# Gate rows computed as columns, diagonal constants moved to VectorE ahead of the loads, last tile's half sums on GpSimd, new priorities and addresses, in an eight-core hybrid trunk layer

## The chip, the cores and the metric

The kernel runs on all 8 cores of one Trainium2 chip. Each core computes one denoising request (1024 latent tokens) and two context requests (2 x 256 tokens); all cores run the same program and exchange nothing. The metric is the device time in microseconds of the slowest core. Before the change it is 719.71 us, the median of 3 runs (719.04 to 720.16).

Each core has a matrix engine (TensorE, PE), VectorE (DVE), ScalarE (ACT), GpSimd (POOL) and SyncE (SP). SP does nothing but issue DMAs. POOL computes and also issues the DMAs that convert float32 weights to bfloat16 on the way.

## What is computed

One layer of a flow-matching backbone. With `mod = silu(cond) @ w_ada + b_ada` split in six vectors of 1024 (shift1, scale1, gate1, shift2, scale2, gate2):

```python
h    = x * (1 + sc1) + sh1
proj = h @ w_in                          # q,k,v,g of 4 retention heads; z,x,B,C,dt of the SSD heads
ret  = silu(g) * rms_norm(bidirectional retention(q, k, v))     # latent q,k get a 2D rotary
ssd  = rms_norm(bidirectional SSD(silu(conv5(x,B,C)), dt) * silu(z)) * ssd_norm_w
x    = LN1(ALPHA * x + g1 * (concat(ret, ssd) @ w_out))
x    = LN2(ALPHA * x + g2 * ((silu(h2 @ w_gate) * (h2 @ w_up)) @ w_down)),  h2 = x * (1 + sc2) + sh2
```

Context tokens (group GA, tiles 8 to 11) use one shared conditioning vector, latent tokens (group GB, tiles 0 to 7) their own. So every modulation vector exists twice per core.

## The kernel before, in words

**The program is a list that a planner orders.** The Python code creates operations (class `Op`) in program order, each with the engines that may run it, a cost in us, a priority (`P.level`, lower goes first, corrected by the table `LEVELS` under the stage's name and level) and its dependencies. Dependencies on SBUF are kept in cells of 32 bytes (`View.cells`). `Prog.schedule` then plays the program with these costs: at each moment an engine takes the ready operation with the lowest priority number. What comes out is a fixed order for every engine; on the chip each engine works through its own list and waits on semaphores. A matmul that takes a new PSUM bank also waits for whatever else the readers of that bank need (`Prog.whole`), so that a bank is never held by something that can't be drained. In the planner's clock a DMA queue moves 318 KB per us (SP) or 290 KB per us (POOL).

**Addresses.** `Prog.place` gives every buffer an address. Two buffers may share bytes if their lifetimes in the planner's time don't meet, with a margin `slack` in us; `PLACED` is a list of addresses tried first. The first operation on a later buffer waits for all operations on the earlier one.

**Stages in order.**
- Start (tag "start"): SP loads, in this order, `cols` (per-partition constants), two halves of `w_ada` slab 2, the first half of `xT` chunk 2 (the context tokens, transposed), of `w_in` slab 0, then `cst` (396 columns: identity, triangle, ones, small tables), the first half of `w_in` slab 1, of `xT` 0, `smalls` (48 values for every partition), `xT` 1, slab 3 of `w_ada`, and the second halves. ACT, DVE and POOL cast the pieces to bfloat16 (L781, L733). `mod_cols` makes scale1 as columns: 32 matmuls with 2 moving columns. The scaled tokens `hA` are then multiplied with `w_in` half by half (`proj_xbc`; the halves are summed on DVE, L756).
- `diagw` (eight 128 x 640) and `dI` (two 128 x 512) are diagonal matrices, made from the identity in `cst` by ten `tt` on DVE or POOL at level 3. `diagw` turns the five-tap convolution into matmuls.
- `sh1` (level 0.6): shift1 as columns from slabs 0 and 1 of `w_ada`, which POOL loads one after the other when `xT` has landed; then shift1 times `w_in` for the bias of the convolution. The convolutions wait for that.
- The context heads, context SSD blocks ("ssd", "blk8" to "blk11"), `gate_row(0, half)` for gate1, `mod2` for shift2 and scale2, the context output stage ("out1"), and then the latent SSD ("ssdB", "blk0" to "blk7"), the latent heads ("head0", which need the rotary table `rope`, 1 MB, loaded by SP behind the last context head), "out0".
- The feed-forward of the latent tokens from 447 us on, in it `gate_row(1, half)`; then the down projection, first the context tiles, then the latent ones, tile 7 last through `last_tile` in column slices of 512, 256 and 256.

**What the change touches.** `gate_row` computes a gate as a row: 8 matmuls with 2 stationary columns (`scv3`) and 512 moving ones, a DVE add of the bias row `gb` (its own SP DMA, which waits for the `w_ada` slab), and a 2 x 512 store into the DRAM scratch `gsc`. `gate_load` reads one 1024-wide row of `gsc` back, broadcast to all partitions, for each group. In `last_tile`, when slice 1 is done, two `ts` on 128 x 1 values (L762, L764) add the two first sums and sums of squares on DVE. In `down` the layer norm's multiply and add (`ln2`) go to POOL, except for tiles 5 and 6, where the planner may choose DVE. `tt` is L756, `ts` L762/L764, `stt` L770, `cp` L781, matmuls L708, transposes L711, DMAs L194.

## Time and profile before

| | us |
|---|---|
| median of 3 runs | 719.71 (719.04 to 720.16) |
| the profiled execution, its own time | 724.19 |
| its span on the slowest core (core 5) | 723.1 |
| spans of the eight cores | 711.1 to 723.1 |
| PE busy (share of the span) | 673.9 (93%) |
| DVE, POOL, ACT busy | 401.2 (55%), 343.7 (48%), 328.2 (45%) |
| DMA share in 0 to 90 us | 0.8 to 1.0 |

The span runs from a core's first to its last instruction; 1.1 us of the profiled execution lie around it. All cores run the same instructions in the same order, so a difference between cores is a difference in when DMAs land.

### The profile page before, as it was taken

How to read it: one execution, taken by the hardware profiler on the slowest of the kernel's cores; microseconds unless marked ns; L12 is line 12 of the kernel's file. 1: busy time of each engine (PE TensorE's matmuls, PEld its weight loads, DVE VectorE, ACT ScalarE, POOL GpSimd, SP SyncE). 2: the span in 40 equal slices, each digit the busy share in tenths (PEclk: the TensorE clock that was granted, in tenths of full speed). 3: DMA queues.
4: the chain of work that ended last, by engine and by line, in shares of the span. 5: the costliest groups of instructions: out<-in, count | busy, mean ns of one | idle time of the engine just before them, and what ended most of it. 6: DMA issues, size and time to landing. Idle time of an engine off the chain costs nothing.

```text
span 723.1 us, 13450 instructions; the slowest of 8 cores (711.1 to 723.1 us)
## 1 busy us (share of the span) xinstructions
PE 673.9 (93%) x4270; PEld 347.1 (48%) x4270; DVE 401.2 (55%) x811; ACT 328.2 (45%) x517; POOL 343.7 (48%) x385
## 2 busy tenths in 40 slices
PE   0699899997999999999999999999999999999994
PEld 0244664643548444446565455444444444444442
DVE  2788358661598935787777885212111222475566
ACT  2281876786756535867887536111111110132212
POOL 2520516322614778876773321886481000298752
PEclk9999899998998999999999999999999999999998
DMA  8989996999394499655069637594589954021112
GB/s 233 330 281 151 145 160 115 197 204 250 76 243 108 73 144 177 124 96 101 19 161 215 152 103 180 96 167 80 125 185 158 245 162 80 1 88 59 58 60 87
DMA packets 26677, 102.93 MB, mean 142 GB/s; under 512 B 3168, under 2 KB 7264, under 8 KB 21744
## 3 DMA queue, kind: packets, MB, share of 16 engines
q0 software_dynamic: 11232, 49.83, 41.6%
q1 hardware_dynamic: 15376, 52.24, 22.1%
q8 instruction: 36, 0.59, 0.3%
q14 instruction: 33, 0.27, 0.1%
HBM read 136.40 MB, written 15.48 MB: 210 GB/s over the span
## 4 chain that ended last, share of the span: by engine, by line
PE 79%; DMA 8%; DVE 5%; issue 4%; ACT 2%; POOL 1%; SPq 1%; DVEq 0%; POOLq 0%; ACTq 0%
PE psum L708 77%; DMA arena<-cstf 6%; DVE arena L756 2%; DMA arena<-w_h 2%; ACT arena L733 2%; PE psum L711 2%; DVE arena L770 1%; DVE arena L781 1%; SPq L194 1%; POOL arena L756 1%; DVE arena L790 1%; POOL arena L194 0%; ACT L733 0%; DVE arena L762 0%; DVEq L610 0%
## 5 line engine op out<-in xcount | busy, mean ns | idle before, releaser
L708 PE MATMUL psum<-arena 128*128 128x512 bf16 (+7 forms) x4174 | 663.5, 316 | 38.1 <-ACT arena L733 23.9
L708 PEld LDWEIGHTS psum<-arena 128*128 128x128 bf16 (+2 forms) x4174 | 335.9, 100 | 362.7 <-issue 86.4
L756 POOL TENSOR_TENSOR arena<-arena 128x512 f32<-128x512 f32 (+5 forms) x215 | 272.9, 1286 | 177.8 <-DVE arena L764 70.9
L733 ACT ACTIVATE arena<-psum 128x512 bf16<-128x512 f32 (+3 forms) x208 | 118.5, 579 | 188.6 <-PE psum L708 174.6
L733 ACT ACTIVATE arena<-arena 128x512 bf16<-128x512 f32 (+8 forms) x160 | 109.7, 706 | 164.6 <-DVE arena L770 86.4
L756 DVE TENSOR_TENSOR arena<-arena,psum 128x512 bf16<-128x512 bf16 (+1 forms) x120 | 80.9, 684 | 144.2 <-PE psum L708 131.7
L756 DVE TENSOR_TENSOR arena<-psum,arena 128x512 bf16<-128x512 f32 (+4 forms) x183 | 111.5, 631 | 59.0 <-PE psum L708 55.2
L733 ACT ACT_TABLE_LOAD x52 | 66.7, 1283 | 21.4 <-PE psum L708 11.0
L756 DVE TENSOR_TENSOR arena<-arena 128x1 f32<-128x1 f32 (+9 forms) x105 | 51.8, 502 | 22.2 <-POOL arena L756 13.6
L194 POOL DMA_DIRECT2D arena<-w_gu x44 | 25.9, 588 | 76.0 <-PE psum L708 69.5
L770 DVE SCALAR_TENSOR_TENSOR arena<-arena 128x512 f32<-128x512 f32 (+2 forms) x77 | 52.9, 697 | 5.0 <-DVE arena L756 0.9
L733 ACT ACTIVATE arena<-psum,arena 128x512 bf16<-128x512 f32 (+2 forms) x59 | 37.3, 650 | 13.4 <-PE psum L711 9.1
L781 DVE CAST arena<-psum 128x512 bf16<-128x512 f32 (+1 forms) x35 | 22.1, 649 | 19.3 <-PE psum L708 19.0
L781 POOL CAST arena<-arena 128x2 bf16<-128x2 f32 (+3 forms) x65 | 19.1, 333 | 20.9 <-DMA arena<-w_in 6.6
L790 DVE TENSOR_SCALAR arena<-arena 128x512 f32<-128x512 f32 (+1 forms) x41 | 23.0, 586 | 0.6
L194 POOL DMA_DIRECT2D arena<-w_h x16 | 8.8, 554 | 28.9 <-PE psum L708 19.0
L194 POOL DMA_DIRECT2D arena<-w_down x4 | 2.1, 528 | 40.8 <-PE psum L708 40.4
L764 DVE TENSOR_SCALAR arena<-arena 128x1 f32<-128x1 f32 (+3 forms) x51 | 9.2, 181 | 20.0 <-ACT arena L733 18.6
L1400 DVE COPY_PREDICATED psum<-arena,psum 128x512 f32<-128x512 uint16 x24 | 16.6, 690 | 5.2 <-PE psum L708 4.9
L781 DVE CAST arena<-arena 128x1024 bf16<-128x1024 f32 (+5 forms) x26 | 13.5, 543 | 9.4 <-DMA arena<-w_ada 6.5
L711 PE MATMUL psum<-arena 128*128 128x128 f32 x96 | 14.8, 299 | 0.6 <-DVE arena L790 0.6
L781 DVE COPY arena<-psum 128x512 f32<-128x512 f32 (+3 forms) x19 | 10.2, 544 | 9.1 <-PE psum L708 8.9
(21 smaller groups left out, 71.3 us busy)
## 6 DMA issues: line engine op xcount, KB each, us to landing
arena<-w_gu POOLq DMA_DIRECT2D x44, 512.0 KB, 7.1
arena<-w_ada POOLq DMA_DIRECT2D x10, 1024.0 KB, 11.9
arena<-w_h POOLq DMA_DIRECT2D x16, 512.0 KB, 10.4
arena<-xT SPq DMA_DIRECT2D x6, 1024.0 KB, 26.1
arena<-x SPq DMA_DIRECT2D x12, 512.0 KB, 10.5
arena<-w_down POOLq DMA_DIRECT2D x4, 1408.0 KB, 15.2
y<-arena SPq DMA_DIRECT2D x11, 512.0 KB, 2.6
arena<-w_ada SPq DMA_DIRECT2D x4, 1024.0 KB, 26.3
```

The lines of the kernel that those rows point to most:

```text
L194: o = self.add({eng: (0.9 if eng == POOL else 0.45, lambda e: e.dma_start(out=R(out), in_=R(in_)))}, [in_], [out], after=after)
L708: return P.add({PE: (c, lambda e: e.matmul(R(out), lhsT=R(lhsT), rhs=R(rhs), start=start, stop=stop))}, [lhsT, rhs], [out])
L711: return P.add({PE: (0.12, lambda e: e.transpose(out=R(out), in_=R(in_), identity=R(ident_f)))}, [in_, ident_f], [out])
L733: fn = lambda e: e.activation(out=R(out), in_=R(in_), func=func, **{k: R(v) for k, v in kw.items()})
L756: fn = lambda e: e.tensor_tensor(out=R(out), in0=R(in0), in1=R(in1), op=op)
L764: fn = lambda e: e.tensor_scalar(out=R(out), in0=R(in0), scalar1=R(s1), scalar2=R(s2), op0=op0, op1=op1)
L770: fn = lambda e: e.scalar_tensor_tensor(out=R(out), in0=R(in0), scalar=R(scalar), in1=R(in1), op0=op0, op1=op1, **{k: R(v) for k, v in kw. ...
L781: alts[g] = (vcost(g, out, [in_], "copy"), lambda e: e.tensor_copy(out=R(out), in_=R(in_)))
L790: lambda e: e.tensor_scalar(out=R(out), in0=R(in_), scalar1=R(scale), scalar2=R(bias), op0=ALU.mult, op1=ALU.add))
L1400: P.add({DVE: (0.7, lambda e, eb=eb, ef=ef, mk_=mk_: e.copy_predicated(R(eb), R(mk_), R(ef)))}, [mk_, ef, eb], [eb])
```

## The change

The priorities and addresses are new as a whole (tables cut here). `cst` is loaded in two parts, its identity and `smalls` ahead of everything but `cols`. The ten diagonal products run on DVE only, at level 0.2 in place of 3; the shift1 section is at level 0.35 in place of 0.6. The first margin tried between lifetimes is 2.0 us in place of 0.2. Gates are computed by `mod_cols` (32 matmuls with 2 moving columns, bias from `cols`), transposed by PE to 8 rows of 128, copied and stored; each is loaded back in two halves. The two sums of the last tile are on POOL, and so is all of the final multiply and add.

```diff
-LEVELS = {('blk0', 1.4): -0.05, ..., ('head0', 1.6): -0.1, ..., ('ssdB', 1.4): 0.02, ..., ('z0', 1.55): 0.5, ...}
+LEVELS = {('blk0', 1.4): -0.5, ..., ('head0', 1.6): -0.06, ..., ('ssdB', 1.4): 0.4, ..., ('z0', 1.55): 1.3, ...}
...
-        for cap, slacks in ((None, (0.2,)), (204000, (3.0, 1.0)), ...
+        for cap, slacks in ((None, (2.0,)), (204000, (3.0, 1.0)), ...
...
+    P.dma(SP, cst[:, 0:128], cf_d[:, 0:128])
+    P.dma(SP, smalls, brow(R_SMALL, 48))
     ada_f32(2)
     for q in range(2):
         xT_load(2, q)
         o_w0 = half_load("w_in0", w0, w_in_d[0], q)
         if q == 0:
-            P.dma(SP, cst, cf_d[:, 0:396])
+            P.dma(SP, cst[:, 128:396], cf_d[:, 128:396])
         o_w1 = half_load("w_in1", w1, w_in_d[1], q)
         xT_load(0, q)
         if q == 0:
-            P.dma(SP, smalls, brow(R_SMALL, 48))
             xT_load(1, 0)
...
+        if name[:2] == "gc":
+            gc[(int(name[2]), int(name[3]))] = m
-        tt(m.rearrange("p (f c) -> p f c", c=2), ps.rearrange("p (f c) -> p f c", c=2),
+        tt(m.rearrange("p (c f) -> p f c", c=2) if name[:2] == "gc" else m.rearrange("p (f c) -> p f c", c=2), ps.rearrange("p (f c) -> p f c", c=2),
...
+    P.level = 0.2
     diagw = P.buf("diagw", 8 * 5 * 128, BF16)
...
-           cols[:, ...].to_broadcast([128, 5, 128]), ALU.mult, (DVE, POOL))
+           cols[:, ...].to_broadcast([128, 5, 128]), ALU.mult)
...
-           smalls[:, 32 + h:36 + h].unsqueeze(2).to_broadcast([128, 4, 128]), ALU.mult, (DVE, POOL))
+           smalls[:, 32 + h:36 + h].unsqueeze(2).to_broadcast([128, 4, 128]), ALU.mult)
...
-    P.level = 0.6
+    P.level = 0.35
     for half in range(2):
         sh1[half] = mod_cols("sh1_%d" % half, half, "mod")
...
     def gate_row(which, half):
-        P.level = LV_BG
-        hs = slice(half * 512, half * 512 + 512)
-        gb = P.buf("gb%d%d" % (which, half), 512)
-        r0 = (R_BG1, R_BG2)[which] + half * 512
-        P.dma(SP, gb[0:2, :], rows_d[0:1, r0:r0 + 512].partition_broadcast(2)..., after=[ada[(4, 10)[which]][1]])
-        P.level = 1.2
-        wv = ada[(4, 10)[which] + half][0].rearrange("p (k n) -> p k n", k=8)
-        ps = P.ps("dense")
-        for kt in range(8):
-            o = mm(ps[0:2, :], scv3[:, kt, :], wv[:, kt, :], kt == 0, kt == 7)
-        P.level = LV_EV
-        gs = P.buf("gst%d%d" % (which, half), 512)
-        tt(gs[0:2, 0:512], ps[0:2, :], gb[0:2, :], ALU.add)
-        P.level = LV_BG
-        gdma[(which, half)] = P.dma(SP, gsc_d[which * 2:which * 2 + 2, hs], gs[0:2, 0:512])
+        P.level = 1.2
+        m = mod_cols("gc%d%d" % (which, half), (4, 10)[which] + half, "dense")
+        P.level = 1.2
+        ps = P.ps("dense", 128)
+        o = tr(ps[0:8, :], gc[(which, half)])
+        P.level = LV_EV
+        gs = P.buf("gst%d%d" % (which, half), 128)
+        cp(gs[0:8, :], ps[0:8, :])
+        P.level = LV_BG
+        r = which * 2 + half
+        gdma[(which, half)] = P.dma(SP, gsc_d[r:r + 1, :].rearrange("a (r p) -> (a r) p", p=128), gs[0:8, :])
         return o
...
     def gate_load(which, g, after):
         b = P.buf("gate%d_%d" % (which, g), 1024)
-        r = which * 2 + g
-        P.dma(SP, b, gsc_d[r:r + 1, :].partition_broadcast(128)..., after=[gdma[(which, 0)], gdma[(which, 1)]] + list(after))
+        for half in range(2):
+            r = which * 2 + half
+            P.dma(SP, b[:, half * 512:half * 512 + 512], gsc_d[r:r + 1, g * 512:g * 512 + 512].partition_broadcast(128)..., after=[gdma[(which, half)]] + list(after))
         return b
...
             if i == 1:
-                ts(s[:, 6:7], s[:, 0:1], s[:, 1:2], ALU.add)
-                ts(s[:, 7:8], s[:, 3:4], s[:, 4:5], ALU.add, EPS, ALU.add)
+                ts(s[:, 6:7], s[:, 0:1], s[:, 1:2], ALU.add, eng=(POOL,))
+                ts(s[:, 7:8], s[:, 3:4], s[:, 4:5], ALU.add, EPS, ALU.add, eng=(POOL,))
...
-                e_ = (DVE, POOL) if t >= 5 and g == GB else (POOL,)
+                e_ = (POOL,)
```

## Rows read from the trace of the kernel before

**Rows 1.** The page: the span, and the engines' busy time, share and instructions

```profile
span 723.1 us, 13450 instructions; the slowest of 8 cores (711.1 to 723.1 us)
PE 673.9 (93%) x4270; PEld 347.1 (48%) x4270; DVE 401.2 (55%) x811; ACT 328.2 (45%) x517; POOL 343.7 (48%) x385
```

**Rows 2.** Spans and granted TensorE clock of single cores

```profile
core 0: 711.1 us, clock 0.988
...
core 5: 723.1 us, clock 0.979
...
core 7: 719.8 us, clock 0.983
```

**Rows 3.** Timeline of PE, core 5: start, us, what, [idle before <- releaser]

```profile
20.79 4.99 PE L708 MATMUL psum<-arena 128*128 128x512 bf16 x16 [5.26 <-ACT arena L733]
29.63 41.80 PE L708 MATMUL psum<-arena 128*128 128x512 bf16 x240 [3.85 <-DVE arena L781]
71.95 0.94 PE L708 MATMUL psum<-arena 128*128 128x2 bf16 x32 [0.53 <-DVE arena L756]
74.19 0.95 PE L708 MATMUL psum<-arena 128*128 128x2 bf16 x32 [1.30 <-DVE arena L781]
76.12 7.66 PE L708 MATMUL psum<-arena 128*128 128x8 bf16 x92 [0.98 <-DVE arena L762]
...
176.24 15.61 PE L708 MATMUL psum<-arena 128*128 128x512 bf16 x116 [4.79 <-DMA arena<-cstf]
```

**Rows 4.** Timeline of all engines, core 5, 0 to 60 us

```profile
1.52 0.89 SPq L194 DMA_DIRECT2D arena<-w_ada  x2
...
21.08 6.16 POOL L756 TENSOR_TENSOR arena<-arena 128x640 bf16<-128x640 f32 x4 [16.57 <-DMA arena<-cstf]
...
22.46 5.46 DVE L756 TENSOR_TENSOR arena<-arena 128x640 bf16<-128x640 f32 x3
...
24.19 1.06 ACT L733 ACTIVATE arena<-arena 128x1024 bf16<-128x1024 f32 x1 [3.54 <-DMA arena<-w_in]
...
27.85 1.52 DVE L781 CAST arena<-arena 128x1024 bf16<-128x1024 f32 x1
...
56.90 0.58 POOL L194 DMA_DIRECT2D arena<-w_ada  x1 [5.46 <-DVE arena L756]
```

**Rows 5.** Windows, core 5: us; PE, PEld, DVE, ACT, POOL busy (x); PEclk, DMA share, GB/s

```profile
4.00:20.00 16.00, 0.99 (x32) 0.94 (x32) 4.01 (x13) 4.94 (x7) 0.51 (x2) 1.00 0.93 284
...
29.60:34.00 4.40, 4.37 (x13) 1.69 (x14) 2.70 (x6) 2.10 (x6) 0.89 (x2) 0.61 1.03 341
...
71.40:85.10 13.70, 9.62 (x158) 7.05 (x157) 7.78 (x26) 11.84 (x19) 10.03 (x53) 0.75 0.98 142
```

**Rows 6.** PE's waits, core 7: us in total, times, longest

```profile
PE psum L708 <- DVE arena L781: 4.6, 3, 2.5
...
PE psum L708 <- DMA arena<-cstf: 1.8, 1, 1.8
```

**Rows 7.** Instructions grouped by form, core 5: busy us, mean ns, then idle before

```profile
L756 DVE TENSOR_TENSOR arena<-arena 128x512 bf16<-128x512 f32 x4 | 2.7, 685 | 0.0
```

**Rows 8.** The page, DMA issues: count, KB each, us to landing

```profile
arena<-w_ada POOLq DMA_DIRECT2D x10, 1024.0 KB, 11.9
```

**Rows 9.** Timeline, core 5: weight loads of two gate rows, and a run of transposes

```profile
494.42 3.11 PEld L708 LDWEIGHTS psum<-arena 128*2 128x2 bf16 x16 [0.42 <-issue]
...
443.26 2.00 PE L711 MATMUL psum<-arena 128*128 128x128 f32 x16 [0.64 <-DVE arena L790]
```

**Rows 10.** Timeline of all engines, core 5, 690 to 724 us

```profile
690.18 1.75 DVE L770 SCALAR_TENSOR_TENSOR arena<-arena 128x512 f32<-128x512 f32 x1
...
709.47 3.46 POOL L756 TENSOR_TENSOR arena<-arena 128x512 f32<-128x512 f32 x2 [1.37 <-ACT arena L733]
...
715.17 0.43 DVE L770 SCALAR_TENSOR_TENSOR arena<-arena 128x256 f32<-128x256 f32 x1
```

**Rows 11.** SP's timeline, core 5: the issue of the rotary table

```profile
148.49 1.49 SPq L194 DMA_DIRECT2D arena<-cstf  x1
```

More of the change, by code:

```diff
@@ L534, in emit @@
         extra = None
-        for cap, slacks in ((None, (0.2,)), (204000, (3.0, 1.0)), (196000, (3.0, 1.0)), (188000, (3.0, 1.0, 0.0)), (180000, (1.0, 0.0))):
+        for cap, slacks in ((None, (2.0,)), (204000, (3.0, 1.0)), (196000, (3.0, 1.0)), (188000, (3.0, 1.0, 0.0)), (180000, (1.0, 0.0))):
             order = self.schedule({}, cap)
@@ L970, in build @@
         tt(diagw4[:, ct, :, :], ident_f.unsqueeze(1).to_broadcast([128, 5, 128]),
-           cols[:, C_CONVW + ct * 5:C_CONVW + ct * 5 + 5].unsqueeze(2).to_broadcast([128, 5, 128]), ALU.mult, (DVE, POOL))
+           cols[:, C_CONVW + ct * 5:C_CONVW + ct * 5 + 5].unsqueeze(2).to_broadcast([128, 5, 128]), ALU.mult)
     dI = P.buf("dI", 1024, BF16)
@@ L1577, in gate_load @@
         b = P.buf("gate%d_%d" % (which, g), 1024)
-        r = which * 2 + g
-        P.dma(SP, b, gsc_d[r:r + 1, :].partition_broadcast(128).rearrange("p a n -> p (a n)"), after=[gdma[(which, 0)], gdma[(which, 1)]] + list(after))
+        for half in range(2):
+            r = which * 2 + half
+            P.dma(SP, b[:, half * 512:half * 512 + 512], gsc_d[r:r + 1, g * 512:g * 512 + 512].partition_broadcast(128).rearrange("p a n -> p (a n)"), after=[gdma[(which, half)]] + list(after))
         return b
```

10 lines of the change are left out of this document (4 added, 6 removed), and 8 rows, old and new, of the table LEVELS.

## The prediction

> **What bounds the kernel now.** I read the page first: PE is busy for 673.9 of 723.1 us [rows 1], so nearly all that can be won is in PE's 49 idle us, in matmuls that run at the lower of TensorE's two levels, and in matmuls that need not be there. Next the cores: all run one program, yet core 0 ends at 711.1, core 7 at 719.8 and core 5 at 723.1 us [rows 2]. The metric is the slowest, so what the late cores lose is what counts. Then PE's timeline for where its idle time lies [rows 3]: 3.85 us ahead of 29.63 us behind a cast on DVE, 0.53, 1.30 and 0.98 us in the chain of small matmuls for shift1 (2.81 together), and 4.79 us ahead of 176.24 us behind the rotary table. The last 275 us have hardly a gap until the final chain. Last the timeline around the first hole: ACT starts its half of the cast of `w_in` slab 1 at 24.19 us, so the data was there, but DVE is in three diagonal products from 22.46 for 5.46 us, and its half of the cast starts at 27.85 [rows 4]. PE waits for that half. It then also pays in clock: it had stood idle for 3.85 us, and in 29.6 to 34.0 us the granted clock is 0.61, that is mostly the 1.2 GHz level [rows 5].
>
> **1. The diagonals.** Removed from the place where they hurt: seven products of 640 on DVE and POOL between 21 and 28 us, one more on DVE behind the cast, and two of 512. With them gone the cast starts at about 24.2 and is over by 25.3 with ACT's 1.06 us [rows 4], before PE ends its first burst at 20.79 + 4.99 = 25.8 [rows 3]. The idle 3.85 us go. The clock would not have fallen: at 0.61 in 4.4 us, the share f of time at 1.2 GHz obeys 1 - f/2 = 0.61, f = 0.78, 3.4 us at half speed, 1.7 us of work lost [rows 5]. Together 5.5 us on core 5. On core 7 the longest wait behind such a cast is 2.5 us [rows 6].
> Where do the ten products go? To DVE alone, once the identity lands, some 4 us in. DVE is busy for 4.01 of the 16 us from 4 to 20 [rows 5], so 12 us are free. Their price there: POOL was at the same work when DVE's took 5.46/3 = 1.82 us each; a product of 512 from SBUF alone takes 0.685 [rows 7], so 640 take 0.86. 8 x 0.86 + 2 x 0.69 = 8.3 us fit; at 1.82 (and 1.46 for 512) they would be 17.5 and not fit. I take 0.86, since POOL has 0.51 us of work in that window [rows 5], and keep 17.5 as a bound: 5.5 us over, the whole gain.
>
> **2. The loads ahead.** SP issues two DMAs more before the first `w_ada` half. Two issues took 0.89 us [rows 4], and 88 KB at 284 GB/s [rows 5] are 0.3. Everything in the load-bound start comes 0.9 us later, from the old place of `smalls` on 0.6. I charge 0.7 to PE. Net of step 1 on core 5: 5.5 - 0.7 = 4.8.
>
> **3. What is late next.** The projections then end sooner, and the shift1 chain needs `w_ada` slab 1. Its DMA is issued at 56.90 [rows 4] and such a slab takes 11.9 us [rows 8]: it lands at 68.8. The chain's first half ran until 71.95 - 0.53 = 71.4, so its 32 matmuls (0.94 us) started at 70.5. With the issue unmoved only 70.5 - 68.8 = 1.7 us can be used. But the issue itself had waited 5.46 us for a DVE sum [rows 4], a buffer's reuse behind PE, which moves with PE and with the new addresses. Between 1.7 and 4.8 I take the middle, 3.3.
>
> **4. The shift1 chain at level 0.35.** The split projections have 0.35 to 0.65 in the new table (before 0.38 to 0.5 against 0.62): the small matmuls can now lie between large ones instead of behind all of them. At best the 2.81 idle us go [rows 3]; at worst the planner, which counts on 290 KB per us, puts them ahead of a slab not landed, and PE waits for it: the same amount again. As the slab is the limit by step 3, I take half, 1.4.
>
> **5. Gates.** A gate row costs 8 matmuls of 512: sixteen weight loads span 3.11 us from first to last, so two gates are 3.11 x 16/15 = 3.3 and one 1.65 [rows 9]. As columns it is 32 matmuls in 0.94 [rows 3], and a transpose, 2.00/16 = 0.13 [rows 9]: 1.07. Four gates: 4 x 0.58 = 2.3 us, all on PE, which is full there. The transpose waits for a DVE add, but the planner has large matmuls to put between; without that cover each would cost some 0.5 (the 0.53 of rows 3), 2 us in all, and the gain is gone. The DMAs: four bias rows go, four half loads come; SP is idle most of the time. Nothing.
>
> **6. The tail.** Tile 6's multiply and add leave DVE, whose evacuation of slice 1 was queued behind them; but all four are now on POOL, from 709.47 at 3.46/2 = 1.73 us beside DVE, or less without. The two small sums stand behind them on POOL, and the next `stt` on DVE, at 715.17 [rows 10], writes the same 32-byte cell, so it waits for POOL. POOL is done with them at 709.47 + 4 x 1.73 = 716.4 at worst, and at 714.4 with 1.23 each (its products of 640 took 6.16/4 = 1.54 [rows 4], so 512 take 1.23); with 0.4 for the two sums (as the `stt` of 256, 0.43) that is +1.6 or -0.4 against 715.17. I take 0, between the two: the gain of the freed DVE is given back at POOL's queue.
> A DVE product beside POOL took 1.75 us where 0.69 is its time alone [rows 7, 10]. The Trainium skill ("SBUF — State Buffer", "two separate sides") says that the pair of ports which DVE and GpSimd share is an exclusive lock and the loser waits for the whole instruction; by it, more of POOL's products in the tail make every DVE operation with two SBUF inputs wait out a POOL instruction, and the tail comes out 1.6 us longer, not equal.
>
> **The rest** (priorities of the middle, addresses, a margin of 2.0 us): no row can price it. The kernel's middle has small waits on PE only, except the rotary table's, which has its own case below. I take 0, with 3 us either way.
>
> **Sum.** For the profiled execution, 724.19: - 3.3 - 1.4 - 2.3 = 7.0 less, 717.2. The median, 719.71, has a slowest core like core 7, whose hole is 2.5 in place of 3.85 [rows 3, 6]: 1.3 us less to win. 719.7 - 5.7 = **714.0 us**.
>
> **Rivals.**
> - **More than that (0.25).** The slab's issue moves too (1.5 more), the whole chain is covered (1.4 more), and the clock stays up where the small matmuls had PE starved: 0.75 in 71.4 to 85.1 [rows 5] is half of 13.7 us at 1.2 GHz, and PE was busy for 9.62 of them, so at most 2.4 us. 714.0 - 5.3 = 708.7. For: these small matmuls are what PE had around that fall of the clock. Against: the slab's DMA.
> - **Slower: the rotary table (0.15).** It is issued at 148.49 [rows 11], and PE stood from 171.45 to 176.24 on core 5 [rows 3], 1.8 us on core 7 [rows 6]. PE had come to its first user 23 us after the issue. Latent heads stand at 1.54 in the new table (1.5 before), z at 2.85 (2.05), latent SSD at 1.8 (1.42): work that lay between issue and use may now lie behind it. The price is us for us, plus what the clock loses after such a stand (1.7 as in step 1). It decides if PE arrives more than 5.7 - 1.7 = 4 us sooner, under 19 us after the issue; at 14 us, 9 more idle + 1.7, less 5.7: 724.7. Against: the context output stage (1.15, before 1.3) still comes ahead of the heads.
> - **Nothing to see (0.12).** The start is a matter of loads alone (DMA share 0.93 to 1.03 [rows 5]), slab 1 lands when it did, the gates' transposes wait; the two added issues eat the rest: 719.5.
> - **The diagonals don't fit DVE** (1.82 each), the casts are late from the first slab: about 721, 0.05, in the slower side.
> The forecast itself has 0.43; its own range, 710.5 to 717.
>
> **Numbers.** 0.2% of this time is 1.4 us, about what a measurement can tell from no change. Faster by more: the forecast, the first rival, and a part of the third: 0.75. Same 0.09, slower 0.16. The range holds the forecast and most of the first rival and ends where no change lies: 707.5 to 720.5.
>
> **What would show it.** Right: on every core PE goes through from its first large matmul to about 45 us with no hole over 1 us and a granted clock of 1.00 behind 25 us; DVE has ten products before 20 us at 0.7 to 0.9 each; no matmul with two stationary columns; the waits of 0.5 to 1.3 us near 72 gone; core spans closer together. Wrong: a wait of PE for `w_ada` between 60 and 75, a wait for `cstf` past 4.8 us near 170, DVE casts late in the first 15 us, or a new group of waits between 180 and 450 us worth over 5 us.

## The result, and the profile after

The changed kernel takes **726.83 us** (median of 4 runs, 724.97 to 727.32) against 719.92 (719.04 to 720.16, 4 runs): ratio 1.0087, 95% interval 1.0068 to 1.0107. It is slower by 0.9%; the forecast was 714.0, with 720.5 as the upper end. The profiled execution took 724.97 us, its slowest core is core 7. Here and below, ratios and means leave out executions in which the cores of a die ran at a lower clock and took longer. (In the changed kernel all helper lines are one less: matmul L707, `tt` L755, `cp` L780.)

The page of the changed kernel, beside [rows 1]:

```profile
span 723.9 us, 13671 instructions; the slowest of 8 cores (712.7 to 723.9 us)
PE 670.4 (93%) x4370; PEld 351.2 (49%) x4370; DVE 395.5 (55%) x811; ACT 338.1 (47%) x523; POOL 346.1 (48%) x391
```

PE is busy for 3.5 us less than in [rows 1] (2.0 less than on core 7 before, 672.4) and the span is 0.8 us longer, so the time did not go into PE's work. ACT is busy for 9.9 us more: it loads its tables 60 times in place of 52, 1.28 us each. No run tests what that costs. First the start. Timeline of PE, changed kernel, core 7 (start us, us, what, [idle before <- releaser]):

```profile
16.11 0.99 PE L707 MATMUL psum<-arena 128*128 128x2 bf16 x32 [16.11 <-POOL arena L780]
22.51 44.08 PE L707 MATMUL psum<-arena 128*128 128x512 bf16 x248 [5.41 <-POOL arena L780]
66.75 1.02 PE L707 MATMUL psum<-arena 128*128 128x512 bf16 x4 [0.15 <-DVE arena L755]
67.97 1.80 PE L707 MATMUL psum<-arena 128*128 128x512 bf16 x36 [0.20 <-DVE arena L755]
71.33 0.94 PE L707 MATMUL psum<-arena 128*128 128x2 bf16 x32 [1.56 <-DVE arena L780]
72.89 7.32 PE L707 MATMUL psum<-arena 128*128 128x8 bf16 x90 [0.63 <-ACT arena L732]
```

The hole of [rows 3] is gone: PE goes through for 44.08 us. The bias matmuls (128x8) start at 72.89, before at 76.64 on this core; in the mean of the cores at 71.6 for 74.7. And the diagonals, DVE grouped by form, changed kernel, core 7, 0 to 20 us:

```profile
L755 DVE TENSOR_TENSOR arena<-arena 128x640 bf16<-128x640 f32 x8 | 6.4, 814 | 0.0
```

814 ns each, before PE's first large matmul. Up to here this is as forecast. Of the waits near 72 us, which were to go, 1.56 and 0.63 us are left. Then the middle, PE by windows on core 7 (us; PE busy; PEclk; DMA share; GB/s). Before:

```profile
76.00:148.00 72.00, 69.56 (x650) 0.96 0.91 159
148.00:200.00 52.00, 47.69 (x368) 1.00 0.80 189
200.00:232.00 32.00, 30.44 (x270) 0.89 0.65 172
232.00:300.00 68.00, 66.37 (x405) 1.00 0.74 130
300.00:345.00 45.00, 44.55 (x344) 1.00 0.51 95
```

After:

```profile
76.00:148.00 72.00, 72.00 (x603) 0.98 0.70 125
148.00:200.00 52.00, 46.23 (x462) 0.90 0.97 207
200.00:232.00 32.00, 27.41 (x218) 1.00 0.57 170
232.00:300.00 68.00, 64.30 (x403) 0.92 0.67 123
300.00:345.00 45.00, 42.65 (x332) 1.00 0.37 72
```

Two things are to be seen. DMA work has moved: share 0.70 for 0.91 in the second window, 0.97 for 0.80 in the third. And PE, which had 8.0 us idle from 148 to 345 us (197 less 189.05), now has 16.4, with a lower clock in two windows (0.90 and 0.92 for 1.00) and a higher one in one (1.00 for 0.89). In the mean of the eight cores, waits of PE over 0.15 us from 200 to 353 us add up to 3.1 us before and 11.0 after. Who makes it wait, PE's waits on core 7 from 180 to 460 us, before:

```profile
PE psum L708 <- ACT arena L733: 2.2, 6, 0.7
PE psum L708 <- DVE arena L781: 0.9, 1, 0.9
```

and after:

```profile
PE psum L707 <- DVE arena L780: 4.6, 3, 1.8
PE psum L707 <- DMA arena<-gsc: 4.2, 1, 4.2
PE psum L710 <- DVE arena L789: 2.6, 1, 2.6
PE psum L707 <- DVE arena L755: 1.9, 3, 1.1
PE psum L707 <- DVE arena L789: 1.3, 1, 1.3
```

One is a load (the gate, 4.2 us), four are DVE. Last the tail, all engines, changed kernel, core 7:

```profile
708.99 5.63 POOL L755 TENSOR_TENSOR arena<-arena 128x512 f32<-128x512 f32 x4 [1.37 <-ACT arena L732]
...
711.86 0.42 DVE L755 TENSOR_TENSOR arena<-psum,arena 128x256 f32<-128x256 f32 x1 [0.79 <-PE psum L707]
714.61 0.30 POOL L761 TENSOR_SCALAR arena<-arena 128x1 f32<-128x1 f32 x1
...
715.07 0.29 POOL L763 TENSOR_SCALAR arena<-arena 128x1 f32<-128x1 f32 x1 [0.17 <-POOL arena L761]
715.47 0.43 DVE L769 SCALAR_TENSOR_TENSOR arena<-arena 128x256 f32<-128x256 f32 x1 [3.19 <-POOL arena L763]
```

DVE's last `stt` waits 3.19 us for two 128 x 1 sums on POOL that stand behind tile 6's four products. From PE's end to the end of the span it is 12.0 to 12.2 us on the eight cores, before 10.4 to 10.7.

**A ledger against the plan.** The planner gives both kernels the same length, 707.3 and 707.5 us. So what the chip adds can be read at any point: the time at which POOL issues a weight load, less its time in the plan. This difference is called the lag. The `w_gu` loads as one tile, core 7 (count, ns, first and last start), before and after:

```profile
L194 POOL DMA_DIRECT2D arena<-w_gu x44: 527/591/651, 206.1 to 554.6; - x44
```

```profile
L193 POOL DMA_DIRECT2D arena<-w_gu x44: 527/591/651, 204.3 to 556.8; - x44
```

The plans have these at 195.4 and 538.1, and at 195.6 and 537.4: the lag is 10.7 and 16.5 us before, 8.7 and 19.4 after. The changed kernel is 1.8 us ahead at the first `w_gu` load and 2.2 behind at the last. In the mean of all eight cores, at plan times in us (all such tables below are worked out in this way, from one profile of each kernel):

| lag, us | 83 | 145 | 196 | 232 | 274 | 290 | 350 | 538 |
|---|---|---|---|---|---|---|---|---|
| before | -0.1 | 3.9 | 7.2 | 11.9 | 12.2 | 12.6 | 13.4 | 12.8 |
| changed | -3.4 | 0.5 | 6.1 | 11.7 | 11.8 | 14.7 | 17.7 | 14.6 |

In this pair the changed kernel is 3.3 us ahead at 83 us, 1.1 at 196 and 0.4 at 274; it is 2.1 us behind at 290, 4.3 at 350 and 1.8 at 538, and the tail adds 1.6. The level of such a row moves by some 3 us from one profile of a kernel to the next: e_after_itself, the changed kernel once more, has 9.9 at 196 and 17.8 at 538. Its growth repeats better. From 145 to 196 us it is 3.3 us before and 5.6 and 6.4 in the two profiles of the changed kernel; from 274 to 350 us 1.2 before, 5.9 and 5.6 after; from 350 to 538 us -0.6 before, -3.1 and -3.0 after. So two stretches lose, some 2.7 and 4.5 us. The theories for this: **A**, loads that crowd after 148 us; **B**, small work on DVE that is held up beside POOL, which the plan does not count; and for the parts, that some of them cost what they should give.

### The profile page after: what moved, and what is told of

Read it like the earlier page. It is cut to its first block, busy times and chain, and to the rows that moved or that the text cites. A ratio compares the mean times of both kernels' runs of the same rounds, so it can differ in the third digit from the quotient of the medians.

```text
span 723.9 us, 13671 instructions; the slowest of 8 cores (712.7 to 723.9 us)
## 1 busy us (share of the span) xinstructions
PE 670.4 (93%) x4370; PEld 351.2 (49%) x4370; DVE 395.5 (55%) x811; ACT 338.1 (47%) x523; POOL 346.1 (48%) x391
## 4 chain that ended last, share of the span: by engine, by line
PE 78%; DMA 9%; DVE 4%; issue 4%; ACT 2%; POOL 2%; SPq 1%; DVEq 0%; POOLq 0%; ACTq 0%
PE psum L707 77%; DMA arena<-gsc 3%; DMA arena<-w_in 2%; PE psum L710 2%; DMA arena<-w_out 2%; ACT arena L732 2%; POOL arena L755 2%; DMA arena<-w_ada 2%; DVE arena L755 1%; DVE arena L769 1%; DVE arena L789 1%; SPq L193 1%; ACT L732 1%; DVE arena L780 0%; POOL arena L780 0%
## 5 line engine op out<-in xcount | busy, mean ns | idle before, releaser
L707 PE MATMUL psum<-arena 128*128 128x512 bf16 (+6 forms) x4270 | 658.3, 311 | 38.3 <-POOL arena L780 21.5
L707 PEld LDWEIGHTS psum<-arena 128*128 128x128 bf16 (+1 forms) x4270 | 338.8, 99 | 353.8 <-issue 76.7
L755 POOL TENSOR_TENSOR arena<-arena 128x512 f32<-128x512 f32 (+4 forms) x216 | 271.0, 1269 | 169.5 <-DVE arena L763 63.0
L755 DVE TENSOR_TENSOR arena<-arena,psum 128x512 bf16<-128x512 bf16 (+1 forms) x120 | 81.0, 684 | 147.3 <-PE psum L707 138.3
L755 DVE TENSOR_TENSOR arena<-psum,arena 128x512 f32<-128x512 f32 (+3 forms) x183 | 109.9, 619 | 69.9 <-PE psum L707 62.6
L755 DVE TENSOR_TENSOR arena<-arena 128x1 f32<-128x1 f32 (+8 forms) x104 | 49.1, 488 | 23.3 <-POOL arena L755 14.7
L780 POOL CAST arena<-arena 128x2 bf16<-128x2 f32 (+4 forms) x68 | 23.4, 381 | 39.6 <-DMA arena<-w_ada 19.1
L732 ACT ACTIVATE arena<-psum,arena 128x512 bf16<-128x512 f32 (+2 forms) x56 | 34.1, 645 | 7.0 <-PE psum L710 4.6
L780 DVE CAST arena<-psum 128x512 bf16<-128x512 f32 (+1 forms) x39 | 23.5, 623 | 13.1 <-PE psum L707 12.8
L710 PE MATMUL psum<-arena 128*128 128x128 f32 (+1 forms) x100 | 16.2, 304 | 3.0 <-DVE arena L789 2.6
L780 DVE COPY arena<-psum 128x512 f32<-128x512 f32 (+4 forms) x22 | 10.7, 490 | 13.5 <-PE psum L707 13.3
L710 PEld LDWEIGHTS psum<-arena 128*128 128x128 f32 (+1 forms) x100 | 12.7, 154 | 6.4 <-issue 5.3
## 6 DMA issues: line engine op xcount, KB each, us to landing
arena<-w_ada POOLq DMA_DIRECT2D x10, 1024.0 KB, 11.7
```

The source lines that it names most:

```text
L707: return P.add({PE: (c, lambda e: e.matmul(R(out), lhsT=R(lhsT), rhs=R(rhs), start=start, stop=stop))}, [lhsT, rhs], [out])
L710: return P.add({PE: (0.12, lambda e: e.transpose(out=R(out), in_=R(in_), identity=R(ident_f)))}, [in_, ident_f], [out])
L732: fn = lambda e: e.activation(out=R(out), in_=R(in_), func=func, **{k: R(v) for k, v in kw.items()})
L755: fn = lambda e: e.tensor_tensor(out=R(out), in0=R(in0), in1=R(in1), op=op)
L780: alts[g] = (vcost(g, out, [in_], "copy"), lambda e: e.tensor_copy(out=R(out), in_=R(in_)))
```

## The experiments

Each kernel was compared with the kernel before on its own chip. The ratio is that of the slowest core, as everywhere here. Since the eight cores of one run differ by 10 us and more, the mean of the eight spans, averaged over the runs, is the finer measure; its difference to the kernel before is given as "mean". For single runs it scatters by 0.3 to 1.4 us (standard deviation), so the difference is good to about 0.5, as far as noise goes. What the choice of addresses does comes on top and has a section of its own.

| run | ratio, 95% interval | mean, us |
|---|---|---|
| e_after_itself | 1.0074 (1.0057 to 1.0090) | +6.3 |
| e_after_sums_dve | 1.0086 (1.0055 to 1.0118) | +5.5 |
| e_before_tail | 1.0006 (0.9990 to 1.0022) | +0.8 |
| e_before_affine_pool | 0.9982 (0.9965 to 0.9998) | -1.3 |
| e_after_half_slabs | 1.0057 (1.0037 to 1.0078) | +3.4 |
| e_before_latent_first | 1.0180 (1.0140 to 1.0220) | +11.1 |
| e_before_start | 1.0098 (1.0084 to 1.0112) | +6.9 |
| e_start_old_order | 0.9950 (0.9930 to 0.9969) | -4.2 |
| e_parts_old_order | 0.9965 (0.9949 to 0.9981) | -3.7 |
| e_after_short_pool | 0.9970 (0.9953 to 0.9986) | -2.3 |
| e_before_short_pool | 0.9975 (0.9961 to 0.9990) | -1.9 |
| e_gates_old_order | 0.9999 (0.9979 to 1.0018) | +0.2 |
| e_parts_table_first | 0.9935 (0.9916 to 0.9955) | -5.4 |
| e_diagonals_old_order | 0.9952 (0.9935 to 0.9969) | -3.3 |
| e_best_old_order | 0.9964 (0.9951 to 0.9977) | -2.3 |
| e_before_addresses | 0.9965 (0.9952 to 0.9977) | -2.9 |
| e_parts_addresses | 0.9967 (0.9952 to 0.9981) | -2.4 |
| e_parts_margin | 0.9915 (0.9895 to 0.9935) | -5.9 |

### The tail

```diff
 # e_after_sums_dve: changed kernel
-ts(s[:, 6:7], s[:, 0:1], s[:, 1:2], ALU.add, eng=(POOL,))        # and the sum of squares
+ts(s[:, 6:7], s[:, 0:1], s[:, 1:2], ALU.add)
 # e_before_affine_pool: kernel before; e_before_tail has this and the two sums on POOL
-e_ = (DVE, POOL) if t >= 5 and g == GB else (POOL,)
+e_ = (POOL,)
```

> The changed kernel with the two small sums of the last tile back on VectorE; nothing else moves, PE's order is the same instruction for instruction. Theory A (the sums are a queue problem: the third slice's statistics wait for two sums that stand behind four GpSimd products): the 3.19 us wait of DVE for POOL goes, the tail from the last matmul to the end shrinks from 12.2 to about 9 us, and the median falls by about 3 us, to 723.5 to 724.5. Rival (the tail is bound by the chain square, rsqrt, two passes, DMA anyway, or by the port pair while GpSimd finishes tile 6): less than 0.7 us, 726 to 727.

> The kernel before with all three tail edits (sums on GpSimd, tile 5 and 6 multiply and add on GpSimd alone). PE's order is unchanged. Theory A: slower by 1.7 us, the difference of the two tails in the profiles (12.2 against 10.4 us behind the last matmul): 721.2 to 722. Rival (tail edits are neutral, as the prediction had it; all of the loss lies in the middle): 719.4 to 720.4.

> The kernel before with only the multiply and add of tiles 5 and 6 moved to GpSimd; the sums stay on VectorE. Theory A: faster by about 1.3 us, since DVE no longer holds slice 1's and slice 2's evacuation behind two products of 1.4 to 1.75 us: 718.2 to 719. Rival (DVE and GpSimd block each other, and GpSimd's four products in a row end later than the chain): the same or up to 1.6 us slower.

From PE's end to the end of the span: 9.8 to 10.4 us with the sums back on DVE in the changed kernel (12.0 to 12.2 with them on POOL), 11.4 to 11.5 in the kernel before with all three edits, 9.3 to 9.4 with only the products on POOL (10.4 to 10.7 before). So **POOL's products gain 1.1 us, the sums on POOL cost 2.1**, and the two edits work against each other. The means of the two runs on the kernel before say the same: -1.3 and +0.8, 2.1 apart. DVE, core 2 of e_after_sums_dve, has no wait in front of the last `stt` now, though it takes 0.93 for 0.43 us beside POOL:

```profile
717.18 0.42 DVE L755 TENSOR_TENSOR arena<-psum,arena 128x256 f32<-128x256 f32 x1 [0.72 <-PE psum L707]
717.52 0.20 DVE L761 TENSOR_SCALAR arena<-arena 128x1 f32<-128x1 f32 x1
717.83 0.21 DVE L763 TENSOR_SCALAR arena<-arena 128x1 f32<-128x1 f32 x1
718.15 0.93 DVE L769 SCALAR_TENSOR_TENSOR arena<-arena 128x256 f32<-128x256 f32 x1
```

In the whole time this gain hardly shows (ratio 1.0086 beside 1.0074 and 1.0087, mean +5.5 beside +6.3): that run's lag at 537 us was 20.3, 2.5 more than in e_after_itself, on a chip on which the kernel before was 0.9 us slower. The tail accounts for 1.6 of the changed kernel's 6 to 7 us; the rest is further up.

### The loads

```diff
 # e_after_half_slabs: changed kernel; the plan still counts the whole slab
+if name in ("ada6", "ada7", "ada8"):
+    o.alts = {POOL: (0.9, lambda e: e.dma_start(out=R(b[:, 0:2048]), in_=R(src[:, 0:2048])))}
 # and the 32 matmuls on such a slab read its loaded half twice: the results are other numbers
 # e_before_latent_first: kernel before
-('proj0', 1.32): 0.1      # the other priorities re-tuned to it by the planner's own estimate
+('proj0', 1.32): -0.18
```

> The changed kernel once more, on the chip on which the next three run, so that they have it as a measure beside the kernel before. Its ratio to the kernel before should again be near 1.009, and the mean of its eight cores' spans some 7 us above that of the kernel before.

> The changed kernel with only the first half of w_ada slabs 6, 7 and 8 loaded (the shift and scale columns are computed with the first half of the rows used twice); order, waits and addresses of everything else are the same. Theory A (the loads): the latent group's preparation now goes ahead of the context heads, so loads that before went out from 119 us on go out from 134 us on and crowd into 148 to 200 us, where the DMA engines are full (share 0.97) at 207 GB/s; the waits between 180 and 233 us come from that. Then half the bytes of three slabs (3 x 512 KB less) take the 4.2 us wait for gsc at 190 us away on the cores that have it, the DMA share between 148 and 200 us falls under 0.9, and the kernel gets 3 to 7 us faster than the changed kernel. Theory B (the order of the small work on DVE, ACT and POOL): the waits at 224, 232, 290 and 325 us have nothing to do with loads; then only the gsc wait goes, the others stay, and the time falls by 0 to 3 us.

> The kernel before with the one priority that the traces point to set as in the changed kernel (the latent group's convolution and transposes at 1.14 in place of 1.42, so ahead of the context heads at 1.3), and the other priorities tuned again by the planner's own estimate, which comes to 713.0 us against 707.3 for the kernel before. Theory A (this priority bunches the loads and DMA is then slower than planned): DMA share in 76 to 148 us falls from 0.9 to about 0.7, in 148 to 200 us it rises to 0.95 or more, and the chip adds to the planner's 5.7 us more: 9 to 13 us slower than the kernel before. Theory B (loads are harmless): slower by the planner's 5.7 us or less.

| lag, us | 83 | 145 | 196 | 232 | 274 | 290 | 350 | 538 |
|---|---|---|---|---|---|---|---|---|
| e_after_itself | -1.7 | 3.5 | 9.9 | 15.1 | 15.2 | 17.9 | 20.8 | 17.8 |
| e_after_half_slabs | -1.8 | 2.8 | 6.7 | 12.0 | 12.1 | 14.8 | 17.7 | 14.5 |

With half the bytes of three slabs, 2.9 us come back (mean +3.4 for +6.3, on one chip). The lag rows alone can't say where, since the changed kernel's first profile has the same lags as this run. PE's waits can: from 148 to 200 us they add up to 5.5, 6.0 and 6.3 us in the mean of the cores in three profiles of the changed kernel (e_after_sums_dve is the middle one), and to 3.3 here; from 200 to 353 us to 10.6 to 11.0, and to 11.1 here. PE by windows in that run, core 7 (columns as above):

```profile
76.00:148.00 72.00, 72.00 (x606) 0.98 0.65 121
148.00:200.00 52.00, 48.24 (x467) 0.90 0.87 191
200.00:232.00 32.00, 26.77 (x218) 1.00 0.54 158
```

The share falls from 0.97 to 0.87 and PE is busy for 2.0 us more in that window, but the window behind it is no better. Theory A is right for some 3 us, the low end of what it expected, and B for what lies behind 200 us. A's mechanism was not right: PE's wait for the gate load did not go. Six cores have it here, 1.7 us in the mean of all eight (1.3 to 2.1 in the profiles of the changed kernel); what went are waits behind ACT and DVE. The waits of 1.8, 2.6 and 1.3 us for DVE stood unmoved, as B had said. The same crowd comes when the kernel before takes this priority: in e_before_latent_first, core 1,

```profile
76.00:148.00 72.00, 72.00 (x508) 0.96 0.52 96
148.00:200.00 52.00, 44.97 (x479) 0.88 1.01 214
```

and the chip adds 5.4 us to the planner's 5.7. Its lag is 13.3 us at 201 and 18.7 at 236, before 7.2 and 11.9. But its other priorities are new too, so the 5.4 are not the loads' alone. The DMA share is 0.97 to 1.01 at 207 to 214 GB/s in this stretch; the planner counts on 290 to 318 KB per us.

### DVE beside POOL

```diff
 # in both kernels, for POOL's tt of 512 columns with 196 < planned start < 350
-e.tensor_tensor(out=R(out), in0=R(in0), in1=R(in1), op=op)
+e.tensor_copy(out=R(out), in_=R(in0))
```

This leaves the second operand out of 47 products (36 in the kernel before), so the results are other numbers; order, addresses and waits are the same. Most are products of the latent heads, 32 of the 47 and 26 of the 36. Such a copy took 0.65 us on POOL where a product took 1.1.

> The changed kernel in which 47 products of 512 columns that the plan puts on GpSimd between 196 and 350 us are replaced by a copy of their first input (about half the time, one input in place of two; the results are other numbers, nothing else moves). If the rest of the loss (lag behind the plan growing by 5.3 us between 196 and 232 and by 5.6 us between 273 and 349, in the kernel before by 4.6 and 1.6) comes from VectorE being held up beside GpSimd's products and from waiting for them, then it becomes 3 to 6 us faster than the changed kernel, and the lag between 273 and 349 us grows by under 2.5 us. If it comes from how PE, ACT and VectorE follow each other, the time moves by less than 1.5 us.

> The same replacement in the kernel before (36 products), as the measure for the run with the changed kernel: by the first theory it gains clearly less than the changed kernel does (0 to 2 us), so that the two kernels come closer; by the second, both gain the same.

The changed kernel goes from +6.3 to **-2.3** us, 8.6 us less; the kernel before gets only 1.9 faster. The two kernels, 6 us apart, are then equal (-2.3 and -1.9). The lag grows by 0.5 us from 196 to 232 (5.3 with the products) and by 3.8 from 274 to 349 (5.6 with them), where under 2.5 were expected: the second stretch is only partly explained by this. PE's waits from 200 to 353 us, in the mean of the cores, fall from 10.6 to 5.4 us (in the kernel before from 3.1 to 2.8). DVE grouped by form, 270 to 350 us, core 1 (busy us, mean ns): kernel before,

```profile
L756 DVE TENSOR_TENSOR arena<-arena 128x512 bf16<-128x512 bf16 x6 | 6.2, 1025 | 1.6 <-PE psum L708 1.5
```

e_after_itself,

```profile
L755 DVE TENSOR_TENSOR arena<-arena 128x512 bf16<-128x512 bf16 x8 | 10.8, 1354 | 0.9 <-PE psum L707 0.6
```

e_after_short_pool:

```profile
L757 DVE TENSOR_TENSOR arena<-arena 128x512 bf16<-128x512 bf16 x10 | 8.6, 878 | 0.8 <-PE psum L709 0.6
```

The same product costs 1.03, 1.35 or 0.88 us, and 0.57 in e_before_short_pool: in either kernel it gets faster when POOL has less to do. The planner counts 0.53. A product that reads PSUM takes 0.68 in all four. Small ones suffer as well: from 196 to 240 us, core 1, in e_after_itself and e_after_short_pool,

```profile
L755 DVE TENSOR_TENSOR arena<-arena 128x8 f32<-128x8 f32 x3 | 2.4, 834 | 0.1
```

```profile
L757 DVE TENSOR_TENSOR arena<-arena 128x8 f32<-128x8 f32 x3 | 1.4, 481 | 0.1
```

against 167 ns for such a one from PSUM; in the kernel before the same three took 158 ns. PE waits for the ends of these chains. From 196 to 240 us the changed plan has 8 of the replaced products, the old one 4, and from 270 to 350 us 32 and 23.

The run does two things at once, and they are not told apart. DVE's own work gets faster, and DVE waits less for POOL's results: from 240 to 350 us such waits fall from 7.3 to 0.9 us in the mean of the cores. In the kernel before they are as long (8.4 us), yet PE waits for DVE for only 0.4 us there, 4.9 in the changed kernel. So it is the new order that puts work on which PE waits beside and behind POOL's products.

The Trainium skill ("SBUF — State Buffer", "two separate sides") has DVE and GpSimd share a pair of ports as an exclusive lock. These rows agree in kind: what is slow on DVE reads SBUF, and what reads PSUM keeps its time. Whether each waits for exactly one POOL instruction no run here shows.

### The parts, on the old order

A first run with the new start only had its priorities tuned anew for a planned 707.8 us (before 707.3):

> The kernel before with the new start alone: diagonals on VectorE behind the identity, the two loads moved ahead, the shift1 chain at 0.35; the other priorities tuned again by the planner's estimate, 707.8 us against 707.3 (latent preparation still behind the context heads). If steps 1 to 4 of the prediction are sound and are not given back, it is 3 to 5 us faster than the kernel before in the mean of the cores, PE has no hole over 1 us before 66 us, and the gain seen at 73 us is still there at the end. If a gain at the start is given back later whatever the priorities (buffers and loads come free at the same time as before), the time is within 1.5 us of the kernel before, with new waits between 100 and 350 us.

It came out 6.9 us slower, and neither theory was right. Its lag is 3.9 at 197 us and 8.1 at 274 (before 7.2 and 12.2, so the start's gain is there), and 20.2 at 539. PE by windows, core 1, this run and the kernel before:

```profile
280.00:345.00 65.00, 60.99 (x460) 1.00 0.58 97
345.00:420.00 75.00, 68.77 (x457) 0.95 0.57 121
```

```profile
280.00:345.00 65.00, 64.36 (x484) 1.00 0.54 102
345.00:420.00 75.00, 74.12 (x500) 1.00 0.62 145
```

8.7 us of PE are lost there, 3.79 of them in one wait for a gate load at 395.78; every core has this wait, 1.6 to 5.0 us. The same start on the old order gives -4.2. **A new table of priorities with the same planned length cost 11 us on the chip**, addresses included. To price a part, the order has to be held. So the next kernels carry the order of the kernel before, instruction by instruction and engine by engine; only the part's own operations are placed anew. Each of them has addresses of its own, because its buffers live at other times:

```diff
+if self.mode is None:                  # an operation of the kernel before
+    o.alts = {e_: o.alts[e_]}          # its engine in the old plan
+    o.key = (int(OLD_RANK[i * 3:i * 3 + 3], 36), len(self.ops))
+# schedule(): it also waits for its predecessor in the old order of its engine
```

> The kernel before, in which every instruction keeps the engine and the place in its engine's order that it had in the kernel before, except for the new start: two loads moved ahead, ten diagonal products on VectorE as soon as the identity is there, the shift1 chain as soon as its data is there. The planner gives it 708.1 us against 707.3. If steps 1 to 4 of the prediction are sound and what lost 7 us in the earlier run with the new start was its newly tuned order behind 287 us, this one is 3 to 4.5 us faster than the kernel before in the mean of the cores, and its lag behind the plan is as in the kernel before from 200 us on, less those 3 to 4.5. If a gain at the start is always eaten later (the loads set the pace), it is within 1 us of the kernel before.

> The new start without the shift1 chain: two loads ahead and ten diagonal products on VectorE, order of all else as in the kernel before. By the prediction's steps 1 to 3 it is 2 to 3.3 us faster than the kernel before in the mean of the cores, and the shift1 chain is worth the other 1 to 2 of the 4.2. If the chain was the whole of it (the slab of w_ada sets the pace anyway), it is under 1 us faster.

> The kernel before, order kept, with the gates alone computed as columns and transposed, and the gate loads in halves. Theory P (prediction's step 5): 2.3 us of PE time less, and 1.5 to 2.3 us faster in the mean of the cores. Theory T (the table): PE comes about 1.2 us earlier to the rotary table, whose load is issued behind the gate loads and lands no earlier, so PE waits for it longer than in the kernel before and the time stays within 1 us of it, or up to 1 us over. Theory G (the gates themselves cost): PE waits at the transposes, lag behind the plan is larger already at 140 us, and the time is 1 to 2.5 us over.

> All parts of the change that the prediction put a price on, on the order of the kernel before: new start, shift1 chain, gates as columns, tiles 5 and 6 multiplied and added on GpSimd; the two small sums of the last tile stay on VectorE. The planner gives 707.0 us. If the prediction's steps are right and only its last term (the new order of everything else, taken as 0) was wrong, it is 6 to 8 us faster than the kernel before: 3.5 from the start, 2 from the gates, 1.3 from the tail. If the gates' transposes or the start cost something that the changed kernel's order hides, it is under 3 us faster.

> As the run with all parts on the old order, and SyncE issues the load of the rotary table ahead of the gate loads in place of behind them. By theory T the wait for the table (1.5 to 3.6 us) goes and it is 1.5 to 3 us faster than the run with all parts, 5.5 to 7 us faster than the kernel before in the mean of the cores. By theory G it is as the run with all parts, 3.7 us faster than the kernel before.

```diff
 # e_parts_table_first, on e_parts_old_order: SP issues it ahead of gate_load(0, GA)
+P.mode, P.rank = "moved", 0
 P.dma(SP, rope, cf_d[:, CF_COS:CF_COS + 2048], after=[ev])
```

| lag, us | 83 | 144 | 196 | 234 | 274 | 291 | 353 | 538 | PE waits for the table, 8 cores |
|---|---|---|---|---|---|---|---|---|---|
| e_start_old_order | -1.8 | 1.4 | 3.5 | 7.3 | 7.9 | 8.0 | 8.8 | 7.4 | four cores, 1.0 to 2.9 us |
| e_parts_old_order | -2.3 | -0.1 | 4.7 | 9.5 | 10.3 | 10.4 | 11.2 | 9.4 | all, 1.5 to 3.6 us |
| e_parts_table_first | -2.8 | 0.1 | 2.0 | 7.5 | 7.9 | 8.0 | 8.9 | 6.8 | none |

With the start the kernel is 4.2 us faster, 3.3 without the shift1 chain, and the lead is still there at the end. How much of it belongs to the start itself is open; the next section comes back to it.

With the gates alone the time stays (+0.2), although PE has less to do: it is busy for 3.3 us less in the mean of the cores (666.6 for 669.9). Two waits take this back. One is the table's: PE waits for it on all eight cores, 2.1 to 3.7 us, 2.9 in the mean, where in the kernel before it did on four, 1.2 in the mean of all eight (1.2 to 1.7 in its profile and three more with its order up to there). Timeline of PE, e_parts_old_order, core 1:

```profile
170.00 0.59 PE L733 MATMUL psum<-arena 128*128 128x512 bf16 x2 [2.86 <-DMA arena<-cstf]
```

The other lies at the first two gates. Between 108 and 128 us PE waits for 2.0 to 2.9 us on every core of e_gates_old_order, and not at all in the kernel before. About half of it stands directly ahead of the second transpose, e_gates_old_order, core 5:

```profile
122.41 0.27 PE L736 MATMUL psum<-arena 128*8 128x128 f32 x1 [1.26 <-DVE arena L781]
```

In e_parts_old_order it is 1.2 to 1.8 us, in the changed kernel 0.1 in the mean, whose order has large matmuls between the two. So theory T holds and so does a part of theory G. One load issued ahead of four others on SP's queue takes the table's wait away on every core; the mean is then -5.4 for -3.7, with other addresses and on another chip.

> The version that the runs so far point to: new start and shift1 chain, tiles 5 and 6 multiplied and added on GpSimd, the table's load ahead of the gate loads; gates as rows as before, everything else in the order of the kernel before. 4.2 from the start and 1.3 from the tail, and up to 1 where a core still waited for the table: 5.5 to 6.5 us faster than the kernel before in the mean of the cores, so about 716.5 us on this chip; if the table's load only pushes the gates' back, 4 to 5.5.

This one missed: -2.3, where 5.5 were expected. No core waits for the table, but four wait 2.0 to 3.2 us at 172 us for a store of `oret`, a wait that e_parts_table_first does not have there. That points at addresses.

### The addresses alone

> The kernel before, the same instructions in the same order, with all buffers at other addresses (210 hand-overs to another engine within 1.5 us of the plan, 171 before). If addresses matter, the mean of the cores is off by 0.5 to 2 us, and rather slower; if they don't, within 0.4 us.

> The run with all parts and the table first (5.4 us faster than the kernel before in the mean of the cores, 130 hand-overs within 1.5 us) with other addresses, 203 such hand-overs. If such hand-overs cost, it gains 1 to 3 us less, 2.5 to 4.5; if not, 5 to 5.8 again.

> The same once more, placed with a margin of 1.0 us in place of 0.2: 27 hand-overs within 1.5 us. If they cost, this is the fastest yet, 6 to 8 us faster than the kernel before in the mean of the cores; if they don't, 5 to 5.8 us.

The edit is another `PLACED` table (in e_parts_margin found with a margin of 1.0 us); every engine's order is the same, instruction for instruction. The kernel before gets 2.9 us **faster**; all parts with the table first give -5.4, -2.4 and -5.9 with three sets of addresses. The last two have the same lag up to 144 us (-0.2 and -0.4), and 5.1 and 1.7 at 196, 10.9 and 5.5 at 234. Timeline of PE, e_parts_addresses, core 4:

```profile
168.86 15.14 PE L733 MATMUL psum<-arena 128*128 128x512 bf16 x116 [3.57 <-DMA oret<-arena]
```

By this row a buffer on that path lies where a state for `oret` is still being stored. Seven cores have this wait, 1.9 to 4.8 us, 3.0 in the mean of all eight; with the addresses of e_parts_margin no core has it. That is most of the 3.5 us between the two. The count of hand-overs of a buffer within 1.5 us of the plan does not explain it: 210 of them went with the gain of 2.9 in the kernel before.

**This changes what the start is worth.** In the kernel before POOL issued the second `w_ada` slab for shift1 at 56.90, behind a wait of 5.46 us [rows 4]. With other addresses and nothing of the change that wait is gone, e_before_addresses, core 5:

```profile
51.61 0.53 POOL L210 DMA_DIRECT2D arena<-w_ada  x1 [1.58 <-DMA arena<-xT]
```

In the mean of the cores this issue comes 3.9 us sooner, in the changed kernel 3.5 and in e_start_old_order 2.4. PE's hole is still there, 1.1 to 3.4 us on every core, since the diagonals are where they were:

```profile
27.55 3.61 PE L733 MATMUL psum<-arena 128*128 128x512 bf16 x16 [2.22 <-DVE arena L806]
```

All the same the bias matmuls start at 73.2 in the mean of the cores, 74.6 to 75.5 in four profiles with the old start at the old addresses, 71.5 to 73.5 in the changed kernel and the runs with the new start. By 144 us addresses alone have brought the lag from 3.9 to 0.4; the seven kernels with the new start on the old order have 1.8 to -1.2 there. So half or more of the start's lead can be had by addresses alone. The new start was never tried with the old addresses.

So addresses are worth about 3 us either way, and every total of a single part above is uncertain by as much. What is seen in rows does not rest on the totals: the hole that goes, the table's wait, the wait at the transposes, and the tail. The changed kernel's addresses keep the 2.0 us margin in the plan everywhere, which speaks against them as the cause of its loss; but the chip is up to 22 us behind the plan, and it was not tried with others.

**The fastest version** is e_parts_margin: all priced parts, sums on DVE, the table first, the old order, 715.66 us against 721.29 on the same chip, ratio 0.9915, and so ahead of both kernels. The interval of e_parts_table_first (0.9935) overlaps with its own.

```profile
span 714.9 us, 13565 instructions; the slowest of 8 cores (705.5 to 714.9 us)
PE 664.0 (93%) x4293; PEld 349.4 (49%) x4370; DVE 391.4 (55%) x817; ACT 328.2 (46%) x517; POOL 340.6 (48%) x383
```

## Why the prediction was wrong

**The step that failed is "The rest": "I take 0, with 3 us either way".** All parts together, on the old order and with the sums on DVE, give 3.7 us (2.4 to 5.9 with the table first), somewhat less than the 5.7 forecast; the changed kernel is 6.3 us slower. Less the 2.1 us of the sums, its new order with its addresses costs some 8 us where 0 was taken, uncertain by the 3 us that addresses do. Two causes are shown, and they overlap, so they don't add up: POOL's wide products beside and ahead of DVE work on which PE waits (8.6 us come back with them shortened, 1.9 in the kernel before), and the crowded loads (2.9 us with three slabs halved). How the first divides between DVE being slower and DVE waiting for POOL stays open, as does what the 8 more table loads on ACT cost. The reason given for the 0 was that the old middle has small waits on PE only. That says nothing of the new middle: PE's waits from 200 to 353 us went from 3.1 to 11.0 us. The planner's equal lengths hid it too, since neither effect is in its costs. The prediction named the sign of trouble, "a new group of waits between 180 and 450 us worth over 5 us", and gave it no case of its own.

- **Step 1**, the diagonals: right in what it removes. 0.81 us each (0.86 taken), all before 20 us, no hole, PE at work from 22.5 to 66.6 at a clock of 1.00. Its size was not measured apart from the addresses.
- **Step 2**, the loads ahead: about right. PE's first large burst starts 1.0 us later in the mean of the cores (21.6 for 20.6), 0.7 were charged.
- **Steps 3 and 4**, slab and shift1 chain: 4.7 were taken for both. The lag at 83 us fell by 3.3 (1.6 in e_after_itself), and the start on the old order gave 4.2. The agreement is in part luck: step 3 tied the slab's late issue to PE, but other addresses alone take that wait away, and 2.9 us with it. The chain's share, 1.0 between two runs with different addresses, is not shown. The waits of the chain did not all go: 1.56 and 0.63 us are left.
- **Step 5**, the gates: the work went (no matmul with two stationary columns is left), the time did not, on the old order. It was **mis-sized at 2.3 and measured 0**. Both dangers that the text named came true there: the transposes are not covered at the first two gates (2.5 us, for which 0.5 each had been weighed), and the table's wait grows by 1.7. That rival's condition, PE more than 4 us sooner, was too strict: the wait was on four cores already, so every microsecond counts at once. In the changed kernel itself neither is there; three cores wait for the gate load instead (3.1 to 4.3 us), and what the gates gain in it was not measured.
- **Step 6**, the tail: taken 0, **measured +1.6**, its upper bound. The mechanism (`stt` waits for sums behind POOL's products) was as written. The choice of the middle was the error: DVE had 3.19 us of wait, not a tie.
- **The rivals**: "slower" came true by another mechanism than the one named, and the chances of its two cases, 0.15 and 0.05, add up to more than the 0.16 that was stated. That the diagonals don't fit DVE (721, 0.05) did not happen.

## What to carry to other kernels

When a change brings a new order for everything along with a few local edits, hold the order and measure the edits, with more than one set of addresses; a planner's equal length said nothing within 10 us here, since its costs leave out DVE beside POOL and a full DMA queue. Before matmul time is cut ahead of a load, look which cores already wait for that load, and move the load first. And small results that a chain waits for don't belong behind wide products on another engine (2.1 us here). One profile's timings scatter by some 3 us too; what repeats is where waits stand and how a lag grows.

## What had not been expected of the hardware

- The same DVE product of 512 bf16 columns with both inputs in SBUF took 1.03 us in the kernel before and 1.35 in the changed one, and 0.57 and 0.88 with POOL's products shortened; one of 8 columns took 0.83 and 0.48 in the changed kernel without and with that. A product of 512 with an input in PSUM took 0.68 us in every case.
- Buffer addresses alone, with the same instructions in the same order, moved the mean of the cores by 2.9 us in one kernel and by 3.5 in another (-2.4 and -5.9). In the first a weight load's issue came 3.9 us sooner, in the second a wait for a store of 3.0 us in the mean of the cores went.
- With the DMA share at 0.97 to 1.01 the queues moved 207 to 214 GB/s between 148 and 200 us, where 0.93 had come with 284 at the start [rows 5].
